# Sums beside the convolution's taps, layer norms shared with GpSimd, and six moved waits in a two-block network on one core

## What is computed

```
def conformer_conv(x, w_pw1, b_pw1, dw_w, dw_b, ln_g, ln_b, w_pw2, b_pw2):
    a = x @ w_pw1 + b_pw1
    u = a[..., :D] * sigmoid(a[..., D:])
    u = causal_depthwise_conv(u, dw_w, width=31) + dw_b
    u = silu(layer_norm(u, ln_g, ln_b))
    return u @ w_pw2 + b_pw2
# differential attention: per head (softmax(q1 k1) - lambda * softmax(q2 k2)) v, rms norm, then @ w_o
# h = h + sigmoid(rms_norm(h) @ w_gate) * (p @ w_proj)         gate stage, after each feed-forward layer
for l in range(2):
    h = x * (1 + sc_m) + sh_m
    y = even_mixer(h) if l == 0 else odd_mixer(h)  # even: sparse attention beside a gated short convolution
    x = layer_norm(alpha * x + (1 + g_m) * y)
    h = x * (1 + sc_f) + sh_f
    x = layer_norm(alpha * x + (1 + g_f) * conv_ffn(h))
```

## Time and profile before

| | us |
|---|---|
| median of 3 runs | 2682.78 |
| the three runs | 2680.94 to 2683.56 |
| the profiled execution, its own time | 2682.27 |
| its span, first to last instruction | 2680.4 |
| TensorE busy in it | 2538.5 (95%) |
| VectorE, ScalarE, GpSimd busy | 1507.4, 1041.7, 1098.7 |
| mean granted TensorE clock | 0.981 of full |

### The profile page before, as it was taken

The page is one execution under the profiler, slowest core; times in us unless marked ns, Lnnn a source line. Parts: engine busy times, 40 slices in busy tenths (PEclk is TensorE's granted clock), DMA queues, the critical chain, the costliest instruction groups (busy, mean ns, idle before and its releaser), DMA issues.

```text
span 2680.4 us, 29894 instructions
## 1 busy us (share of the span) xinstructions
PE 2538.5 (95%) x11024; PEld 1984.1 (74%) x11024; DVE 1507.4 (56%) x1936; ACT 1041.7 (39%) x1369; POOL 1098.7 (41%) x378
## 2 busy tenths in 40 slices
PE   7979999998999899999999998999998999899997
PEld 5748888886767578888877866788886646688886
DVE  5985756753444467477439555652654344662553
ACT  5454222234565442123334242642434233642343
POOL 6824444343434244444433453244443243244442
PEclk9989999999999899999999999999999999999999
DMA  5214646533221155554343302233322211233331
GB/s 156 64 37 145 193 143 189 168 93 107 64 75 51 59 170 179 159 188 144 97 120 88 95 32 71 68 86 106 95 82 84 74 49 47 64 92 103 94 86 64
DMA packets 398589, 273.35 MB, mean 102 GB/s; under 512 B 11108, under 2 KB 380772, under 8 KB 398477
## 3 DMA queue, kind: packets, MB, share of 16 engines
q1 hardware_dynamic: 384652, 221.55, 28.8%
q10 hardware_dynamic: 13824, 50.34, 5.1%
HBM read 269.74 MB, written 2.12 MB: 101 GB/s over the span
## 4 chain that ended last, share of the span: by engine, by line
PE 83%; DVE 8%; ACT 4%; issue 2%; POOL 2%; SPq 0%; DMA 0%; DVEq 0%; ACTq 0%; POOLq 0%
PE ps L664 25%; PE ps L665 25%; PE ps L666 25%; DVE ps L1807 2%; PE ps L877 1%; PE ps L947 1%; POOL arena L2064 1%; PE ps L1155 1%; PE ps L862 1%; PE ps L1065 1%; ACT weight_hi L2167 1%; PE ps L972 1%; PE ps L846 1%; PE ps L1165 1%; POOL weight_lo L2051 1%
## 5 line engine op out<-in xcount | busy, mean ns | idle before, releaser
L2051 POOL TENSOR_TENSOR weight_lo<-weight_raw,weight_hi 128x2048 fp32r<-128x2048 f32 (+2 forms) x224 | 921.6, 4115 | 1373.5 <-ACT weight_hi L2167 1372.6
L664 PE MATMUL ps<-u_hi,weight_hi 128*128 128x512 f32 x2336 | 929.8, 398 | 68.5 <-DVE u_lo L1257 43.8
L665 PE MATMUL ps<-u_lo,weight_hi 128*128 128x512 f32 x2336 | 914.6, 392 | 0.0
L666 PE MATMUL ps<-u_hi,weight_lo 128*128 128x512 f32 x2336 | 914.5, 391 | 0.0
L2167 ACT ACTIVATE weight_hi<-weight_raw 128x2048 fp32r<-128x2048 f32 (+2 forms) x224 | 383.1, 1710 | 568.5 <-PE ps L666 534.2
L664 PEld LDWEIGHTS ps<-u_hi,weight_hi 128*128 128x128 f32 x2336 | 442.4, 189 | 180.3 <-DVE u_lo L1257 54.3
L665 PEld LDWEIGHTS ps<-u_lo,weight_hi 128*128 128x128 f32 x2336 | 442.6, 189 | 95.9 <-issue 5.5
L666 PEld LDWEIGHTS ps<-u_hi,weight_lo 128*128 128x128 f32 x2336 | 441.9, 189 | 93.8
L664 PE MATMUL ps<-act_hi,weight_hi 128*128 128x512 f32 x704 | 274.4, 390 | 2.0 <-DVE act_lo L1225 2.0
L665 PE MATMUL ps<-act_lo,weight_hi 128*128 128x512 f32 x704 | 273.9, 389 | 0.0
L666 PE MATMUL ps<-act_hi,weight_lo 128*128 128x512 f32 x704 | 273.9, 389 | 0.0
(11 more groups left out here) (296 smaller groups left out, 2502.7 us busy)
## 6 DMA issues: line engine op xcount, KB each, us to landing
weight_raw<-in_ffn_w_up SPq DMA_DIRECT2D x132, 512.0 KB, 5.3
arena<-in_ada_w ACTq DMA_DIRECT2D x96, 512.0 KB, 5.8
weight_raw<-in_ffn_w_down SPq DMA_DIRECT2D x64, 704.0 KB, 4.5
weight_raw<-in_ffn_w_gate SPq DMA_DIRECT2D x44, 512.0 KB, 4.0
weight_raw<-in_ev_w_in SPq DMA_DIRECT2D x10, 1024.0 KB, 5.8
weight_raw<-in_conv_w_pw SPq DMA_DIRECT2D x16, 512.0 KB, 5.4
weight_raw<-in_ple_w_gate SPq DMA_DIRECT2D x16, 512.0 KB, 3.7
weight_raw<-in_attn_w_qkv SPq DMA_DIRECT2D x16, 512.0 KB, 4.6
```

What stands on the lines that cost most here:

```text
L664: pe.matmul(bank, w[0], x[0], start=start, stop=False)
L665: pe.matmul(bank, w[0], x[1], start=False, stop=False)
L666: return pe.matmul(bank, w[1], x[0], start=False, stop=stop)
L2051: pool.tensor_tensor(w_lo[r][:, 0:width], raw[r][:, 0:width], w_hi[(k0 + j) % HI_RING][:, 0:width].bitcast(F32), ALU.subtract).then_inc(w_ ...
```

## The change

1. **Convolution.** Chunk 6 gets 7 taps on TensorE instead of 5, chunk 7 gets 20 instead of 18; VectorE does as many fewer. The sums over the chunks go to bank 1; those of chunks 0 to 5 stand before chunk 7's taps, those of 6 and 7 behind.
2. **Layer norms.** TensorE does both partial sums before the last chunk. ScalarE copies the scaled mean to SBUF (`mean_copied`); in three of the mixer norms its split of a weight slot moves from before the mean to behind this copy. VectorE makes the variance in PSUM at once and then centres chunks 0 to 3; GpSimd centres chunks 4 to 7 (`centred`). ScalarE writes the new `h` after all operands.
3. **First query/key slot.** It waits for two tiles fewer, the rms statistic stands before chunk 6 instead of 5, VectorE adds before it sums, and ScalarE's last split of the gate stage stands before the last gate.
4. **Diff attention's end.** VectorE and ScalarE finish head 5 in step 9, behind the copies of head 7's transposes. The third `wo` slot is split into the region of `act_hi`, in step 9. The last `wo` slot is interleaved and counts `x_free`; the operands of the next stage are made as after `pw2`.
5. **Second gate stage.** ScalarE's last split stands before the last operand instead of behind it.
6. **Sparse attention.** The second `e_gate` slot stands behind head 0's scores, and its two tiles are gated by VectorE behind head 0's maxima; the gated operands are split one or two heads later.

The diff's core:

```diff
-PE_TAPS = (5, 5, 5, 5, 5, 5, 5, 18)
+PE_TAPS = (5, 5, 5, 5, 5, 5, 7, 20)
...
     for k in range(len(loads)):
-        hi_free.append(last_use[k % HI_RING])
-        if split_no[k]:
+        third_wo = k == stages["wo"][0] + 2
+        hi_free.append(0 if third_wo else last_use[k % HI_RING])
+        if split_no[k] and not third_wo:
             last_use[k % HI_RING] = tiles_after[k]
...
+        def w_hi(k):
+            return act_hi[:, 0:SLOT] if k == third_wo else hi_ring[k % HI_RING]
...
                 n.take(summed, DC - 1)
-                for c, x in enumerate(chunks):
-                    pe.wait_ge(h_ready, c + 1)
-                    pe.matmul(ps[:, 4], ones, x, start=c == 0, stop=False)
-                if not chunks:
-                    pe.wait_ge(sums_ready, n.next(sums_ready))
-                    pe.matmul(ps[:, 4], ones, sum1, start=True, stop=False)
+                pe.wait_ge(sums_ready, n.next(sums_ready))
+                pe.matmul(ps[:, 4], ones, sum1, start=True, stop=False)
+                pe.wait_ge(sums_ready, n.next(sums_ready))
+                pe.matmul(ps[:, 5], ones, sum2, start=True, stop=False)
                 chunk_made()
                 pe.matmul(ps[:, 4], ones, last_chunk, start=False, stop=True).then_inc(stat_done, 1)
+                pe.wait_ge(squared, n.next(squared, DC))
+                pe.matmul(ps[:, 5], ones, sq[1], start=False, stop=True).then_inc(var_stat, 1)
...
-                if kind == "dsa":
-                    pe.wait_ge(tile_used, stages["e_out"][2] + BANKS)
...
-                        pe.wait_ge(tile_used, BANKS + (first if t0 == first else t0 + i - 1))
+                        pe.wait_ge(tile_used, BANKS + (first - 2 if t0 == first else t0 + i - 1))
...
-                            if k == 5:
+                            if k == 6:
                                 rms_stat()
...
+                w = slot_of("wo", Step(3))
+                banks = [open_tile(first_wo, Step(3), 2, i) for i in range(2)]
+                for k in range(DC):
                     for i in range(2):
-                        bank = open_tile(first_wo, Step(j), 2, i)
-                        for k in range(DC):
-                            mm = product(bank, plain_cols(w, i, k), xu(k), k == 0, k == DC - 1)
-                        mm.then_inc(tile_done, 1)
+                        mm = product(banks[i], plain_cols(w, i, k), xu(k), k == 0, k == DC - 1)
+                        if k == DC - 1:
+                            mm.then_inc(tile_done, 1)
+                    if k < DC - 1:
+                        mm.then_inc(x_free, 1)
...
             stage_gemm("pw1", behind=lambda c: pe_taps(c - 1) if c else None)
+            pe.wait_ge(tile_used, BANKS + 14)
+            for c in range(DC - 2):
+                pe.wait_ge(h_ready, c + 1)
+                pe.matmul(ps[:, 1], ones, chunk(conv_out, c), start=c == 0, stop=False)
             pe_taps(DC - 1)
-            pe.wait_ge(pe_taps_used, DC - 1)
-            ln_stat(chunk(conv_out, DC - 1), lambda: pe.wait_ge(h_ready, DC), [chunk(conv_out, c) for c in range(DC - 1)])
+            conv_stat()
...
-            stage_gemm("e_gate", wait=False)
+            gate_slot(0)
...
-            attention("dsa")
+            def gate_behind_scores():
+                gate_slot(1)
+                pe.wait_ge(tile_used, stages["e_out"][2] + BANKS)
+            attention("dsa", gate_behind_scores)
...
                 dve.wait_ge(mean_done, n.next(mean_done))
-                centre(0)
-                centre(1)
                 dve.wait_ge(var_stat, n.next(var_stat))
-                link(dve.scalar_tensor_tensor(var, ps[:, 5], 1.0 / D, rinv[1], ALU.mult, ALU.subtract))
+                link(dve.scalar_tensor_tensor(var, var, 1.0 / D, rinv[1], ALU.mult, ALU.subtract))
                 link(dve.tensor_scalar(var, var, 0.0, None, ALU.max))
                 dve.sem_inc(var_done, 1)
-                centre(2)
-                centre(3)
+                dve.wait_ge(mean_copied, n.next(mean_copied))
+                for c in range(DC // 2):
+                    link(dve.scalar_tensor_tensor(chunk(src, c), mean, -1.0 / D, chunk(src, c), ALU.mult, ALU.add))
                 dve.wait_ge(rinv_done, n.next(rinv_done))
                 for c in range(DC):
+                    if c >= DC // 2:
+                        dve.wait_ge(centred, c0 + c - DC // 2 + 1)
                     dve.tensor_tensor(chunk(src, c), chunk(src, c), root, ALU.mult).then_inc(xn_ready, 1)
-                    if c + 4 < DC:
-                        centre(c + 4)
...
-                    early = DC - 2 if name == "pw2" else 0 if name == "wo" else DC
+                    early = DC - 2 if name in ("pw2", "wo") else DC
...
                     scale(j)
+                    add(j)
                     if sums and j:
                         sums_add(j - 1, base)
-                    add(j)
...
+                    if i == G + 1:
+                        finish(G - 3)
                     if 0 <= i - 2 < G:
                         dve.wait_ge(o_done, i - 1)
...
+            def centre(src):
+                means[0] += 1
+                pool.wait_ge(mean_copied, means[0])
+                for c in range(DC // 2, DC):
+                    pool.tensor_tensor(chunk(src, c), chunk(src, c), sum1, ALU.add).then_inc(centred, 1)
...
+                elif name in ("up2a", "o_in", "up3a"):
+                    low_halves(name, 0, 1)
+                    centre(h)
+                    low_halves(name, 1, slots)
...
+                sc.activation(sum1, ps[:, mean_bank(src)], ACT.Copy, scale=-1.0 / D).then_inc(mean_copied, 1)
+                if beside:
+                    beside()
                 sc.wait_ge(var_done, n.next(var_done))
...
-                    if then and 1 <= c <= 4:
-                        then(c - 1)
                 if then:
-                    for c in range(4, DC):
+                    for c in range(DC):
                         then(c)
...
+                def third_split():
+                    sc.wait_ge(x_ready, x0 + 4)
+                    split(third_wo)
...
+                    if i == G + 1:
+                        finished(G - 3)
+                        third_split()
...
                     operand_half(DC - 2)
+                    split_after("ple1", Step(DC - 1))
                     sc.wait_ge(tile_used, BANKS + t0 + 2 * DC)
                     operand_half(DC - 1)
-                    split_after("ple1", Step(DC - 1))
...
+                split_after("ple0", Step(DC - 1))
                 gate(Step(DC - 1))
...
             def gated_high(g, first=y0):
-                if g == 0:
+                if g in (1, 2):
```

128 lines of the change are left out of this document (75 added, 53 removed).

## The result

| | before | changed |
|---|---|---|
| median of all runs next to each other | 2681.94 us (4 runs, 2680.94 to 2683.56) | 2649.38 us (4 runs, 2645.40 to 2657.68) |
| ratio, 95% interval | | 0.9882, 0.9858 to 0.9906 |
| profiled execution, its own time | 2682.27 us | 2657.68 us |
| its span | 2680.4 us | 2655.9 us |

The change takes 32.6 us off; the forecast was 38.8 us off the median shown then (2644 us). The profiled execution of the changed kernel is the longest of its four, so a second profile of it (run `again`, span 2647.6 us) stands beside the first in what follows.

The account below looks back on a forecast made before the run. TensorE, busy 95% of the span, was taken as the bound, so only its idle time and clock loss count. Terms summed to -38.4 us: 2682.3 - 38.4 + 0.5 = 2644 us, range 2630 to 2660.

Parts of the forecast that it names:

- Convolution, -1.2: Convolution's end: moved taps and earlier sums fill TensorE's idle time and VectorE has fewer taps left; -1.2 us.
- -2.7 and +0.4: Ends of the range at the convolution: -2.7 us if TensorE's clock stays up, +0.4 us if it falls.
- The norm's loop: Norm behind the convolution: its loop was to give 0.7 us, counted where the clock stays up.
- First query/key slot, -3.5: First query/key slot: it starts earlier with its bound lowered by two tiles, the statistic becoming the next limit; -3.5 us.
- the stall it priced: First query/key slot: VectorE's sixth operand subtraction is held by GpSimd's 4.6 us; without that stall, -9.2 us.
- Diff attention's end and output product, -15.4: Head 5's finish behind the copies, third output slot split early, last slot interleaved; -15.4 us, ends -9 and -16.5.
- Cover A: Output product: one 4.5 us idle time with half clock stays; +8 us, 2652 to 2656 us; chance 0.18.
- Index product, -4.2: Index product: the split ahead of the last operand starts 2.8 us earlier, shrinking idle time and half clock; -4.2 us.
- Gate slot, +2.2: Sparse attention: gate slot behind head 0's scores starts the chain 3.15 us later, normalising gives back 0.97; +2.2 us.
- Norms, -4.2, -5.3, -4.2, -2.6: Four layer norms: split, centrings and stalled maximum leave the path, loops run faster; gains in us as listed.
- rival C: Norms: GpSimd's centring becomes their path if one addition takes over 4 us; near 2688 us; chance 0.04.
- Rival B: GpSimd misses the sixth subtraction, the convolution's clock holds, the gate slot costs nothing; about 2635 us; chance 0.17.

Follow-up runs that it names:

- again: The changed kernel once more, unchanged, for a second profile: 2649.4 us (12 runs).
- gate_slot_back: Changed kernel with the first ada loads issued earlier and the sparse attention's second gate slot back ahead of head 0's scores: 2644.49 us.
- third_ring: Changed kernel with the first ada loads issued earlier and the output product's third slot split into its old ring place again: 2656.22 us.
- qk_split_back: Changed kernel with the first ada loads issued earlier and ScalarE's last split of the first gate stage back behind the last operand: 2644.23 us.
- split_front: Changed kernel with the first ada loads issued earlier and ScalarE's weight split ahead of the mean's square again in three norms: 2649.84 us.
- taps_back: Changed kernel with the first ada loads issued earlier and TensorE's taps of chunks 6 and 7 back at 5 and 18: 2649.56 us.

## Why the prediction was right, point by point

**The whole** came 5.4 us above the forecast and inside the range. Two runs settle parts of it by themselves (`gate_slot_back`, `third_ring`), and `qk_split_back` and `split_front` settle causes; head 5's finish, the interleaved last slot and the index product rest on the stretches of the table alone. The terms of the edited parts behind the convolution add up to -37.2 in the forecast and -38.7 in the table; the difference to the result is the convolution and the unedited stretches.

**Convolution, -1.2: the step that failed.** Seven profiles have the changed kernel's code here. From the first product to the norm's first product, against 160.50 us before (162.34 in the second profile of before), they have -0.4 us where the clock held (two), +0.7 in the first profile, where it fell in part, and +2.5 to +3.0 in four. Part of this is not the change: the way from the first product to chunk 0's gate varies from 13.4 to 14.8 us in both kernels. From chunk 0's gate to the norm's first product the kernel before has 146.9 and 147.6 us, the changed one 146.1 with the clock held, 147.8 in part and 148.8 fallen. So against the first profile the ends are -0.8 and +1.8, where the prediction had -2.7 and +0.4. The order of events is the one described; the term was mis-sized:
- VectorE waits less, but the last chunk comes 1.05 us earlier and not 1.33, since the twenty taps took 17.44 us and not 17.2 (from chunk 7's gate to chunk 7's end 21.86 us in `again`, 22.91 before).
- Of it 0.4 us go back at chunk 3. I had called the larger diagonals hidden in GpSimd's idle time. In `again` the last of them take 4.47 us, in `taps_back` 4.05; GpSimd's next subtraction starts 0.4 us later, and VectorE's first own tap of the chunk, which has two SBUF sources, is held 3.40 instead of 2.97 us.
- The norm's loop gave 0.1 us (7.97 against 8.07 of idle time), not 0.7.
- The fallen clock costs the 2.65 us I had worked out (5.49 against 2.84), but it falls in most executions, and I had taken the middle between falling and not.
- The terms that the prediction names (1.33 for the taps, 0.7 for the loop) add up to -2.0 for the clock that holds; for the rest of its -2.7 it gives no price, and the runs show none.
- Another 0.9 us of the +2.7 in the table lie before chunk 0's gate (14.5 us from the first product in `again`, 13.6 in the first profile of before, 13.4 in that of the changed kernel), where nothing was changed.

**First query/key slot, -3.5:** -3.0. The mechanism is the one described, with a second stall in front of it that I left out. That the sum comes out near is in part luck: without the stall it priced it gave -9.2, and the run without that stall has -6.5 at the head sums, most of which is gone at the first value slot.

**Diff attention's end and output product, -15.4:** -16.1, of which -6.9 for the finish moved behind the copies (-5.2 against the second profile of before, where the clock recovered sooner) and -9.2 for the rest; the ring place alone is 6.4 by `third_ring`. Cover A was there: no idle time at slot 2 or 3.

**Index product, -4.2:** -4.4. **Gate slot, +2.2:** +2.1, with both of its halves measured. This was the one part forecast as a loss, and it is one.

**Norms, -4.2, -5.3, -4.2, -2.6:** -4.8, -5.4, -4.8, -2.3. The idle time fell to 7.85 us and not to 8.5, and 1.43 us are new at the third up slot, as foretold. The reason given first, the 1.89 us of the split in front of the mean's square, is the smaller one: 0.2 to 0.8 us. So here the size was right and the weight of its causes was not. GpSimd's four centrings took 4.95 us, 1.2 each, against the 4 each from which rival C would have decided.

**Rival B** was right in one thing, that the clock at the convolution's end can hold, and wrong in the other two. Of **rival D** little was seen: the freed gaps that reappeared behind a later engine are the foretold one at the third up slot and the 2.42 us behind VectorE at the first value slot (in `again`, but in neither first profile). Two figures of the prediction do not follow from its own terms: its lower ends add up to 2629 us and not 2630, and with the 12 us a norm of rival C three norms would end near 2694 us and not 2688. Neither bears on the forecast.

## What to carry to other kernels

When an operation that waits for a load has two SBUF sources and a long GpSimd operation is due beside it, look at which starts first and by how much: with the margins of 0.30 to 0.48 us above, executions of one kernel fell on either side, and the loss can repeat from slot to slot. Issuing the load early widened the margin to 2.0 us here; that it shortens the median was not shown. An idle time of TensorE is worth its length plus the clock behind it only if the work behind it can run at full clock: fill it with spare products where three sums follow, not where operands arrive more slowly than products. Of a split that is moved, ask which wait of its engine it can stand in, and which GpSimd subtraction it then sets off beside which VectorE operation.
